# Reordering the gated reads, the small normalisation and one weight rounding in the mixer's tail of a hybrid transformer block

## The reference

```python
def hybrid_mixer(n, ...):
    proj = n @ w_in
    aq, ak, av, az, aa, ab, bq, bk, bv, iq, ik, iw = jnp.split(proj, SPLIT_POINTS, axis=-1)
    o_a = gated_deltanet(aq, ak, av, az, aa, ab, conv_a, a_log, dt_bias, a_out_norm)
    o_b = dsa_attention(bq, bk, bv, iq, ik, iw, q_norm, k_norm, kidx_norm, ...)
    gates = jax.nn.sigmoid(n @ w_gate + b_gate).reshape(Bsz, T, 2, D)
    y = gates[:, :, 0] * (o_a @ w_branch_a) + gates[:, :, 1] * (o_b @ w_branch_b)
    return y @ w_out
# gated_deltanet, for each chunk of tokens:
#   v_new = u - w S;  o = q S + (q k^T) v_new;  S = S * decay + k^T v_new
# dsa_attention, for each block of queries: a top-64 choice of keys by an index score,
#   p = softmax(q k^T over the chosen keys);  o = p v
```

## Time and profile before

| | |
|---|---|
| median of three executions | 1622.48 us |
| the profiled execution | 1624.33 us |
| its span, first to last instruction | 1622.5 us |
| TensorE busy | 1583.8 us (98%) |
| VectorE busy | 1178.0 us (73%) |
| ScalarE busy | 904.1 us (56%) |
| chain that ended last | TensorE 81%, VectorE 11%, ScalarE 4% |
| granted TensorE clock, mean | 0.991 |

### The profile page before, as it was taken

The page is one execution under the profiler, slowest core; times in us unless marked ns, Lnnn a source line. Parts: engine busy times, 40 slices in busy tenths (PEclk is TensorE's granted clock), DMA queues, the critical chain, the costliest instruction groups (busy, mean ns, idle before and its releaser), DMA issues.

```text
span 1622.5 us, 34719 instructions
## 1 busy us (share of the span) xinstructions
PE 1583.8 (98%) x12673; PEld 1546.3 (95%) x12673; DVE 1178.0 (73%) x1929; ACT 904.1 (56%) x1419; POOL 71.1 (4%) x62
## 2 busy tenths in 40 slices
PE   8998999999999989999999999999999999999998
PEld 7988989999999879899999989999999999999998
DVE  7778877766559689787665667888756746678863
ACT  5664565655546745656554555666545455566642
POOL 3111001000000101000000000000000000000000
PEclk9998999999999989999999999999999999999999
DMA  6633335555555432365656544566656535646553
GB/s 204 208 103 99 105 116 170 165 182 171 175 163 163 138 103 92 114 191 183 209 182 190 166 155 145 154 196 185 190 183 189 171 119 156 182 152 197 183 184 113
DMA packets 272207, 261.41 MB, mean 161 GB/s; under 512 B 20009, under 2 KB 270533, under 8 KB 272115
## 3 DMA queue, kind: packets, MB, share of 16 engines
q1 hardware_dynamic: 270547, 256.15, 50.9%
q0 software_dynamic: 1376, 3.87, 0.8%
q10 hardware_dynamic: 192, 0.14, 0.0%
HBM read 256.70 MB, written 3.42 MB: 160 GB/s over the span
## 4 chain that ended last, share of the span: by engine, by line
PE 81%; DVE 11%; ACT 4%; issue 2%; DMA 2%; SPq 1%; DVEq 0%; ACTq 0%
PE lin L551 22%; PE lin L554 22%; PE lin L559 22%; PE aux L899 5%; PE lin L899 3%; PE lin L605 3%; DVE wL L538 2%; PE lin L576 1%; ACT wH L529 1%; DVE cT L2075 1%; DMA stage<-in_w_gate 1%; DVE nT L2530 1%; DVE nT L2026 1%; DVE nL L2535 1%; PE lin L636 1%
## 5 line engine op out<-in xcount | busy, mean ns | idle before, releaser
L529 ACT ACTIVATE wH<-stage 128x1024 fp32r<-128x1024 f32 x488 | 493.7, 1049 | 481.9 <-PE lin L554 333.9
L538 DVE TENSOR_TENSOR wL<-stage,wH 128x1024 fp32r<-128x1024 f32 x488 | 580.1, 1231 | 142.2 <-PE lin L559 85.7
L551 PE MATMUL lin<-nH,wH 128*128 128x256 f32 (+2 forms) x2256 | 559.8, 287 | 1.4 <-DVE u L2579 0.7
L554 PE MATMUL lin<-nL,wH 128*128 128x256 f32 (+2 forms) x2256 | 554.7, 285 | 0.0
L551 PEld LDWEIGHTS lin<-nH,wH 128*128 128x128 f32 x2256 | 425.5, 189 | 4.7 <-issue 2.2
L554 PEld LDWEIGHTS lin<-nL,wH 128*128 128x128 f32 x2256 | 426.6, 189 | 1.1 <-issue 0.7
L559 PE MATMUL lin<-nH,wL 128*128 128x256 f32 (+2 forms) x2256 | 295.0, 283 | 0.6 <-DVE wL L538 0.6
L559 PEld LDWEIGHTS lin<-nH,wL 128*128 128x128 f32 x2256 | 281.4, 188 | 1.1 <-DVE wL L538 1.1
L551 PE MATMUL lin<-aH,wH 128*128 128x256 f32 (+1 forms) x704 | 172.3, 284 | 0.0
L554 PE MATMUL lin<-aL,wH 128*128 128x256 f32 (+1 forms) x704 | 172.2, 284 | 0.0
L551 PEld LDWEIGHTS lin<-aH,wH 128*128 128x128 f32 x704 | 132.8, 189 | 0.0
(11 more groups left out here) (416 smaller groups left out, 2202.4 us busy)
## 6 DMA issues: line engine op xcount, KB each, us to landing
stage<-in_w_up SPq DMA_DIRECT2D x88, 512.0 KB, 4.7
stage<-in_ffn_w_up SPq DMA_DIRECT2D x88, 512.0 KB, 4.1
stage<-in_w_in SPq DMA_DIRECT2D x52, 512.0 KB, 4.8
stage<-in_w_down SPq DMA_DIRECT2D x40, 512.0 KB, 3.7
stage<-in_ffn_w_down SPq DMA_DIRECT2D x40, 512.0 KB, 4.2
stage<-in_w_gate SPq DMA_DIRECT2D x32, 512.0 KB, 4.4
stage<-in_even_w_in SPq DMA_DIRECT2D x24, 512.0 KB, 4.6
stage<-in_w_out SPq DMA_DIRECT2D x16, 512.0 KB, 4.1
```

Of the source, the lines that this page charges most:

```text
L529: nc.scalar.activation(wH[:, s, ks, 0:n], stage[:, s, ks, 0:n], ACT.Copy).then_inc(sem["whi"], 1)
L538: nc.vector.tensor_tensor(wL[:, s, ks, 0:n], stage[:, s, ks, 0:n], wH[:, s, ks, 0:n].bitcast(F32), ALU.subtract).then_inc(sem["wlo"], 1)
L551: mm = nc.tensor.matmul(banks[b][0:rows_, 0:width], wH[:, s, k, cols], xh, start=start and n == 0, stop=False)
L554: mm = nc.tensor.matmul(banks[b][0:rows_, 0:width], wH[:, s, k, cols], xl, start=False, stop=False)
```

## The change

Three calls on VectorE move to later places, one pair is swapped, and one call on ScalarE moves ahead of two others. Nothing is added or removed.

```diff
@@ ScalarE
                 weights_turned(1)
                 gate(2)
                 softmax(2)
+                gate_hi(3, [0])
                 delta_out(1)
                 weighted_values(1)
-                gate_hi(3, [0])
                 weights_turned(2)
@@ VectorE
                 greatest(0)
                 biased()
-                gate_lo(2, [0])
-                normed(0)
                 state(0)
                 greatest(1)
                 inverse_ready(1)
                 inverse_ready(2)
+                normed(0)
                 unseen_values(1)
+                gate_lo(2, [0])
+                normed(1)
+                gate_lo(2, [1])
                 split_lo(dve, m0 + M_GATE + 3, 0)
-                gate_lo(2, [1])
-                normed(1)
                 out_lo(0)
                 gate_lo(3, [0])
                 greatest(2)
                 gated(0)
                 state(1)
                 normed(2)
+                out_lo(1)
                 unseen_values(2)
-                out_lo(1)
                 gated(1)
```

## The result

The changed kernel took 1632.38 us (median of 6 runs, 1628.20 to 1636.25) against 1620.97 us for the kernel before on the same chips (6 runs, 1618.73 to 1624.33): a ratio of 1.0068, 95% interval 1.005 to 1.0086. It is slower by 11.4 us. The forecast was 10.7 us more, 1633.2 us in all. Fifteen executions of the changed kernel are recorded with this result, the profiled one among them: 1627.79 to 1637.38 us, with a median of 1631.49, which is 10.5 us more.

What follows compares the result with a forecast made beforehand. TensorE, busy nearly all of 1622.5 us, was taken as the bound. A first stall of 4.0 us plus 1.37 gave 5.4 a layer, 10.7 for two layers: 1633.2 us, range 1629.5 to 1638.

Steps and rivals of the forecast that it cites:

- Step 1: VectorE ahead of state(0): removing two calls only lengthens the 1.30 us idle time by their 1.2 us; gain zero.
- Steps 2 and 3: TensorE waits 1.70 us for normed(0), then 1.20 for the bank gate_lo(2,[0]) empties; gate(3,[0]) starts 2.97 us late.
- Step 4: split_lo behind normed(1) makes wL 3.25 us late, replacing the 2.97; the later branch panel DMA stays covered.
- Step 5: After TensorE's stall in gate(3,[0]) the clock falls to half; 0.75 us taken, between nothing and 1.04.
- steps 2 to 5: First stall of TensorE in each layer: 3.25 us for late wL plus 0.75 for the clock, 4.0 us.
- Steps 6 and 7: ScalarE's moved gate_hi(3,[0]) delays out_lo(1), and unseen_values(2) queues behind it: new_values(2) 1.37 us late per layer.
- R1: Clock stays up after the first stall: 4.6 us a layer, 9.2 in all, 1631.7 us; chance 0.15.
- R2: Clock falls a second time in each layer, after step 6's stall: 3.0 us more in both, 1636.2; chance 0.27.
- R3: Not slower: TensorE does not wait for the moved calls, gaining 0.9 us a layer, 1620.7 us; chance 0.04.
- R4: Delay absorbed by a DMA wait after gate(3,[1]): costs under 3 us, about 1623.5 us; chance 0.06.
- The sum for the weight loads: If weights load during waits, an estimated 0.11 us comes off each of three stalls per layer: 10.0 us in all.

Runs made afterwards that it cites:

- VectorE's part alone: Changed kernel with ScalarE's gate_hi(3,[0]) back behind weighted_values(1), as in the kernel before: 1628.96 us, ratio 1.005 to the kernel before.
- the two calls back in place: Changed kernel with gate_lo(2,[0]) and normed(0) put back ahead of state(0) on VectorE: 1629.87 us, ratio 1.0057 to the kernel before.

## Why the prediction was right

**Step 1** held: the idle time ahead of `state(0)` became 2.43 us, and nothing behind it started earlier.

**Steps 2 and 3** held to some hundredths where no low clock comes before them: waits of 1.74 and 1.20 us (1.70 and 1.20 forecast), the gate panel 3.07 and 3.04 late with VectorE's part alone (2.97). Taking either call alone showed that each is a wait of its own, and putting both back removed both.

**Step 4** held at full clock, but seldom counts. The wait for wL of 0.66 us shows only where the clock stays up, which it did in one of the four stretches of the changed kernel. With the two calls back in place the same order is the main loss (wL 1.9 and 1.8 us late). SyncE's later issue of the branch panel was indeed hidden: ScalarE took the panel at 209.92 without a wait.

**Step 5** was right in kind, and its total was mis-sized; that 10.7 came so near to 11.4 is in part luck. At vn1 the changed kernel was 4.94 and 4.72 us late, in its second profile 4.39 and 4.83, where steps 2 to 5 gave 4.0. At full clock 3.25 is due, so the clock took 1.1 to 1.7 and not 0.75. Where `gate(3,[0])` had one low stretch, the term itself was well sized: gate3 to wL took 5.58, 5.41 and 5.61 us against 4.79 at full clock, so 0.6 to 0.8 (the 1.70 it was worked out from is too much by itself, 1.3 was measured with `normed(0)` late). Two things were missing. `joined(6)` can run at the low clock; `inverse_ready` and with it `normed(0)` are then late by up to 1.1 us. And the low stretch in `gate(3,[0])` was twice as long in 3 of the 8 stretches in which TensorE stood for both calls (it fell in 7 of the 8). In these three it fell 7.1 to 7.6 us into the stretch, before the second wait was over. Step 5 says that this costs less; it cost 1.6 and 1.9 us in the two that can be compared. As the kernel before also loses 1.1 us whenever `joined(6)` is slow, the first of these would not change the difference of the medians much if it is as frequent in both. The few profiles can't show whether it is (3 of 4 stretches of the changed kernel, 1 of 4 of the one before).

**Steps 6 and 7** held: vn1 to vn2 takes 13.69 and 13.62 us in place of 12.21 and 12.20, so 1.48 and 1.42 more (1.37 forecast). The move of ScalarE's call makes the swap on VectorE useless: alone, the swap brings 0.4 us; alone, the call costs 0.8; together 1.4 to 1.5, as R now queues behind an `out_lo(1)` that waits.

**Nothing was seen to be given back** behind the stretch: the changed kernel's two profiles have stretches of 76.9 and 76.4 us for both layers, the kernel before's two 64.2 and 65.3. The means differ by 11.9 us, the medians of the runs by 11.4. The time outside the stretch scatters by 6 us between profiles, so a give-back of a few microseconds can't be told from it.

**The rivals.** R1, the clock stays up, happened once in four stretches of the changed kernel, but even there `joined(6)` was slow, and wL was 4.39 us late and not 3.25. The rule of the Trainium skill that the prediction cites for it (TensorE: Matmul & The Clock Gate, HAM oscillation) would keep the clock up in all of them. The trace does not agree: it fell in 7 of the 8 stretches with both waits, none of which is longer than 1.74 us. Nor does the wait's length decide by itself, as the clock stayed up after 2.67. R2, a second fall after the stall for `o1`, is refuted: in the eight stretches with that wait of 1.5 us the clock never fell. R3 is refuted by the waits shown, R4 by the 11.4 us, as it allows under 3. The sum for the weight loads, 10.0 us, should be 10.1 (10.74 less six times 0.107). Of the weight loads: they did not go ahead of the waits. Queue of weight loads of the changed kernel, first layer:

```profile
192.51 0.17 PEld L1150 LDWEIGHTS aux<-c,P 16*16 16x16 f32 x4 [1.19 <-issue]
193.95 0.29 PEld L551 LDWEIGHTS lin<-nH,wH 128*128 128x128 f32 x1 [1.28 <-issue]
```

The loads start 0.03 us ahead of their matmuls at 192.54 and 193.98, after the wait. The rule of the Trainium skill on loads pulled ahead (TensorE: Matmul & The Clock Gate, Step-by-step: what each phase is for) speaks of matmuls in flight, and gains nothing here across a semaphore wait.

## What to carry to other kernels

In a list that an engine works off in order, look for its idle times that end on another engine's product: work placed ahead of them is free as long as it fits in, and moving it behind them puts it on the path of whoever asks next. Of every call that is moved later, ask for both of its results, the value and the bank or buffer that it empties; here the bank cost more than the value. Don't add up the prices of the parts, or take one part back and call the difference its price: two moves can make the same product late, and then taking back either one brings less than it costs alone. Where two engines' lists are changed together, work out the second with the first already changed: a swap that gained 0.4 us alone led to a loss behind ScalarE's new order.

## What the runs showed of the hardware that was not expected

The granted clock fell to 0.5 with no idle time of TensorE before it, in `joined(6)`, in 9 of 24 stretches of kernels whose TensorE list is the same. Ahead of it stand small products with only 16 of the 128 rows in use (`16x16` and `16x128`, 184.75 in the changed kernel), and after them `scores(1)`, which uses all 128. After a stand it is no more regular: full clock after 2.67 and 2.16 us, half clock after 1.73 in one layer and not in the other. Whether the small products have to do with the falls in `joined(6)` was not tried; the cause is open. Such a fall is worth 1.1 to 1.5 us, and with some of them in an execution it is a likely source of the scatter of 5 to 8 us between runs. The record agrees for the changed kernel: of its fifteen executions the two slowest (1636.25 and 1637.38 us) have a mean granted clock of 0.988, the three fastest (1627.79 to 1630.21) one of 0.994 or 0.995. For a TensorE that is always busy, 0.006 less of the mean clock would be 0.6% more time, 10 us (an estimate from these figures); the means of the two groups lie 8.1 us apart. In other kernels here the tie is looser.
